# Decoder layer on one core: a weight block meets 520 tokens in matmuls of 402, 354, 284, 284 and 236 columns instead of six of 260

## What is computed

```python
xn = _rmsnorm(x, n_mix_pre)
q, fp, iv, og, lx, ly, ga, gb = jnp.split(xn @ w_in, idx, axis=-1)
f = lbh + (1.0 - lbh) * jax.nn.sigmoid(fp)
o, S_new = _hgrn2(silu(q), 1.0 - f, iv, jnp.log(f), S0, chunk)
o = o * lax.rsqrt(jnp.mean(o * o, axis=-1, keepdims=True) + EPS) * hg_onorm * silu(og)
out_a = o @ w_pa
xc, cbuf_new = _causal_conv(lx, cbuf, conv_w, conv_b)
h, h_last = _rglru(xc, xb @ wa + ba, xb @ wx + bx, log_lambda, h0, fresh)
out_b = (jax.nn.gelu(ly) * h) @ w_pb
merged = sigmoid(ga) * out_a + sigmoid(gb) * out_b
x = x + _rmsnorm(merged @ w_o, n_mix_post)
gate, up = jnp.split(_rmsnorm(x, n_ffn_pre) @ w_fi, 2, axis=-1)
x = x + _rmsnorm((silu(gate) * up) @ w_fo, n_ffn_post)
```

## Time and profile before

| | us |
|---|---|
| median of 3 runs | 1100.99 (1100.98 to 1101.19) |
| span of the profiled execution, first to last instruction | 1098.3 |
| TensorE busy, share | 1055.9, 96% |
| its weight loads | 1034.8, 94% |
| VectorE | 573.2, 52% |
| ScalarE | 434.1, 40% |

### The profile page before, as it was taken

One profiled execution on the slowest core, in us unless ns is written; L12 is line 12 of the kernel. 1 busy time (PEld: TensorE's weight loads), 2 busy tenths in 40 slices (PEclk: granted clock), 3 DMA queues, 4 the chain that ended last, 5 costly groups with the idle time before them and its releaser, 6 DMA issues.

```text
span 1098.3 us, 21670 instructions
## 1 busy us (share of the span) xinstructions
PE 1055.9 (96%) x8542; PEld 1034.8 (94%) x8542; DVE 573.2 (52%) x1028; ACT 434.1 (40%) x588; POOL 2.9 (0%) x9
## 2 busy tenths in 40 slices
PE   4899999999999999999999999699999999999997
PEld 3799999999999899999999999699999999999997
DVE  2666566657656788833333333855554554422223
ACT  5434335433442888822222233652323232322222
POOL 0000000000000000000000000000000000000000
PEclk9999999999999899999999999899999999999999
DMA  5533223222332233232333244033233323233321
GB/s 155 162 90 99 79 76 98 86 76 76 94 108 60 81 93 86 78 95 81 91 95 95 88 130 135 20 97 95 80 92 95 95 82 90 67 92 94 94 76 78
DMA packets 182881, 100.36 MB, mean 91 GB/s; under 512 B 3709, under 2 KB 181378, under 8 KB 182594
## 3 DMA queue, kind: packets, MB, share of 16 engines
q1 hardware_dynamic: 164898, 90.87, 27.8%
q10 hardware_dynamic: 17792, 8.91, 2.7%
q0 software_dynamic: 160, 0.15, 0.0%
HBM read 90.79 MB, written 9.13 MB: 91 GB/s over the span
## 4 chain that ended last, share of the span: by engine, by line
PE 90%; DVE 3%; ACT 2%; issue 1%; SPq 1%; DMA 1%; DVEq 0%; ACTq 0%
PE proj L1223 78%; PE pr L1322 5%; PE pi L1371 1%; DMA raw<-in_w_in 1%; PE pr L1376 1%; PE pi L1353 1%; PE pr L1345 1%; PE pi L1414 1%; PE pr L1414 1%; PE pi L1359 0%; ACT wh L358 0%; SPq L266 0%; DVE tmp L1122 0%; DVE acts L1110 0%; DVE raw L1202 0%
## 5 line engine op out<-in xcount | busy, mean ns | idle before, releaser
L1223 PE MATMUL proj<-acts,wh 128*128 128x260 f32 x4928 | 810.7, 287 | 15.5 <-DVE acts L1110 9.2
L1223 PEld LDWEIGHTS proj<-acts,wh 128*128 128x128 f32 x4928 | 679.9, 190 | 23.7 <-DVE acts L1110 10.8
L1223 PE MATMUL proj<-acts,wl 128*128 128x260 f32 x2464 | 498.5, 284 | 0.0
L1223 PEld LDWEIGHTS proj<-acts,wl 128*128 128x128 f32 x2464 | 381.9, 190 | 0.0
L720 DVE TENSOR_TENSOR wl<-raw,wh 128x1024 fp32r<-128x1024 f32 (+2 forms) x164 | 190.8, 1163 | 278.7 <-ACT wh L358 278.6
L358 ACT ACTIVATE wh<-raw 128x1024 fp32r<-128x1024 f32 (+2 forms) x164 | 165.6, 1010 | 358.9 <-PE proj L1223 350.5
L1322 PE MATMUL pr<-tmp 128*128 128x64 f32 (+1 forms) x512 | 66.4, 272 | 3.2 <-DVE tmp L947 3.2
L1322 PEld LDWEIGHTS pr<-tmp 128*128 128x128 f32 x512 | 62.9, 192 | 4.0 <-DVE tmp L947 3.4
L805 DVE TENSOR_TENSOR tmp<-tmp 128x256 f32<-128x256 f32 x56 | 23.6, 422 | 25.5 <-PE pr L1322 25.4
L676 ACT ACTIVATE acts<-tmp 128x520 f32 (+1 forms) x21 | 13.4, 639 | 42.4 <-DVE tmp L1170 42.4
L673 ACT ACTIVATE tmp<-tmp 128x520 f32<-128x520 f32 x21 | 13.5, 641 | 40.0 <-DVE tmp L1161 40.0
(11 more groups left out here) (239 smaller groups left out, 721.0 us busy)
## 6 DMA issues: line engine op xcount, KB each, us to landing
raw<-in_w_in SPq DMA_DIRECT2D x64, 512.0 KB, 4.0
raw<-in_w_ffn_in SPq DMA_DIRECT2D x44, 512.0 KB, 3.8
raw<-in_w_ffn_out SPq DMA_DIRECT2D x16, 384.0 KB, 3.1
raw<-in_w_ffn_out SPq DMA_DIRECT2D x16, 320.0 KB, 2.9
tmp<-in_state_hgrn ACTq DMA_DIRECT2D x8, 512.0 KB, 4.1
out<-tmp ACTq DMA_DIRECT2D x8, 512.0 KB, 3.2
raw<-in_w_branch_a SPq DMA_DIRECT2D x8, 512.0 KB, 3.6
raw<-in_w_branch_b SPq DMA_DIRECT2D x8, 512.0 KB, 3.5
```

The lines of the kernel that those rows point to most:

```text
L1223: o = mm(pp[par][:, hf, 0:TH], w, x[:, hf * TH:(hf + 1) * TH], start=start and n == 0, stop=stop and n == 2)
```

## The change

It cuts the 520 tokens at MA = 284 into an early part and a late part of MB = 236, twice MS = 118. A tile of activations with its low parts is now one row of 1040 columns: low parts of tokens 284 to 401 (118), the high parts (520), low parts of tokens 402 to 519 (118), low parts of tokens 0 to 283 (284). A matmul of 402 columns takes the first low piece with the early high parts, one of 354 the late high parts with the second low piece, one of 284 the early low parts; then the low weights meet the high parts in 284 and 236 columns. The results of the 236 late low columns land beside the others, in **side columns** of the bank pair (all four banks are one tensor now). They are added later: ScalarE's `keep_side` copies them to SBUF, VectorE's `gather` adds them to the late columns and says `summed`; all readers wait for that in place of `unit_done`.

A unit now does its eight k-tiles with the high weights first (waiting for `hi_ready` alone), then waits for `lo_ready` and does the eight with the low weights. A new word, `high_done`, falls between. ScalarE's prep waits for `high_done` and `lo_ready` of two units before, in place of `unit_done`; VectorE's prep waits for `unit_done` of two units before as well. The small matmuls stand at the same four points in the time of a unit. Low parts of activations are made by two VectorE instructions (284 and 2 x 118 columns) instead of one of 520. In the recurrent stage and the output projection ScalarE's prep is moved ahead of the reader of the unit. The masks are cast in one instruction of 576 columns, and broadcast where they are used.

```diff
+MA = 284
+MB = T - MA
+MS = MB // 2
+SW = MS + T
...
-        masks = sb("masks", [P, TP + (NLEV - 1) * TP // 2], U8)
+        masks = sb("masks", [P, MW], U8)
+        side = sb("side", [P, 2, MB])
...
                 if not isinstance(u, int) or u >= 2:
-                    eng.wait_ge(E("unit_done"), u - 1)
+                    eng.wait_ge(E("high_done"), u - 1)
+                    eng.wait_ge(E("lo_ready"), u - 1)
                 act(wh[:, s % 2, 0:nk], raw[:, s, 0:nk], AF.Copy).then_inc(E("hi_ready"), 1)
+            def keep_side(u, par, n=None):
+                n = u if n is None else n
+                eng.wait_ge(E("unit_done"), u + 1)
+                if not isinstance(n, int) or n >= 2:
+                    eng.wait_ge(E("summed"), n - 1)
+                act(side_copy(par), proj_side(par), AF.Copy).then_inc(E("side_kept"), 1)
...
+                    prep(u0 + 2 * bb + 1, 2 * bb + 1)
+                    keep_side(u0 + 2 * bb - 1, 1)
                     squares_of_ly(n - 1)
-                    prep(u0 + 2 * bb + 1, 2 * bb + 1)
                     gelu_tanh(n - 1)
                     branch_high(n - 2)
                     gates(n - 1)
                     prep(u0 + 2 * bb + 2, (2 * bb + 2) % 4)
+                    keep_side(u0 + 2 * bb, 0)
                     pre_conv(n, u0 + 2 * bb)
...
                 eng.wait_ge(E("hi_ready"), u + 1)
+                if not isinstance(u, int) or u >= 2:
+                    eng.wait_ge(E("unit_done"), u - 1)
                 tt(wl[:, s % 2, 0:nk], raw[:, s, 0:nk], wh[:, s % 2, 0:nk].bitcast(F32), SUB).then_inc(E("lo_ready"), 1)
+            def gather(u, par, n=None):
+                eng.wait_ge(E("side_kept"), (u if n is None else n) + 1)
+                eng.wait_ge(E("unit_done"), u + 1)
+                tt(proj_late(par), proj_late(par), side_copy(par), ADD).then_inc(E("summed"), 1)
+            def low_parts(reg, j, x):
+                h = hi_of(reg, j).bitcast(F32)
+                tt(lo_early(reg, j), x[:, 0:MA], h[:, 0:MA], SUB)
+                return tt(lo_late(reg, j), late(x), late(h), SUB)
...
-            for i in range(NLEV):
...
-                cp(mask(i).rearrange("p (c n) -> p c n", c=NCH), src).then_inc(E("m_made"), 1)
+            cp(masks[:], raw[:, 3].rearrange("p k n -> p (k n)")[:, 0:MW]).then_inc(E("m_made"), 1)
...
-            def ktile(s, par, reg, k, start, stop, koff=0):
...
+            def high_weights(s, par, reg, k, start, koff=0):
+                w = wh[:, s % 2, k, :]
+                columns(par, w, reg, koff + k, 0, MS + MA, -MA - MS, start, False)
+                columns(par, w, reg, koff + k, MS + MA, MB + MS, 0, start, False)
+                return columns(par, w, reg, koff + k, SW + MS, MA, -MA, False, False)
+            def low_weights(s, par, reg, k, stop, koff=0):
+                w = wl[:, s % 2, k, :]
+                columns(par, w, reg, koff + k, MS, MA, -MA, False, stop)
+                return columns(par, w, reg, koff + k, MS + MA, MB, 0, False, stop)
...
-                eng.wait_ge(E("lo_ready"), u + 1)
+                eng.wait_ge(E("hi_ready"), u + 1)
...
                 for k in range(nk):
                     if ready:
                         ready(k)
-                    o = ktile(s, par, reg, k, first and k == 0, last and k == nk - 1, koff)
+                    o = high_weights(s, par, reg, k, first and k == 0, koff)
+                    if k == nk - 1:
+                        o.then_inc(E("high_done"), 1)
+                    if k in (2, 5):
+                        for f in fill.get(k // 3, ()):
+                            f()
+                eng.wait_ge(E("lo_ready"), u + 1)
+                for k in range(nk):
+                    o = low_weights(s, par, reg, k, last and k == nk - 1, koff)
                     if k == nk - 1:
                         o.then_inc(E("unit_done"), 1)
```

More of the change, by code:

```diff
@@ L565, in _ @@
             first_tap(0)
+            prep(u0 + 3, 3)
             eng.wait_ge(E("p_os"), NH)
+            keep_side(u0 + 1, 1)
             squares_of_ly(0)
-            prep(u0 + 3, 3)
             squares(h)
@@ L573, in _ @@
             out_high(h)
+            prep(u0 + 4, 0)
+            keep_side(u0 + 2, 0)
             pre_conv(1, u0 + 2)
-            prep(u0 + 4, 0)
             gates(0)
@@ L593, in _ @@
                 ch.end(Q_LRU - 1)
+            prep(4 * G_MIX + 1, 1)
+            keep_side(4 * G_MIX - 1, 1)
             squares_of_ly(NH - 1)
-            prep(4 * G_MIX + 1, 1)
             gelu_tanh(NH - 1)
@@ L655, in _ @@
             prep(4 * G_FFI + 2, 2)
+            keep_side(4 * G_FFI, 0)
+            keep_side(4 * G_FFI + 1, 1)
             inverse_rms(1, 0)
@@ L670, in ffi @@
                     prep(u0 + 2 * jj + 2, (2 * jj + 2) % 4)
+                    keep_side(u0 + 2 * jj, 0)
                     eng.wait_ge(E("d_slr"), j)
@@ L913, in hg_steps @@
                 if prev:
+                    gather(4 * h - 1, 1)
                     prep(4 * h + 1, 1)
@@ L920, in hg_steps @@
                     level(h - 1, 7)
+                gather(4 * h, 0)
                 prep(4 * h + 2, 2)
@@ L928, in hg_steps @@
                     chunk_states(h - 1)
+                gather(4 * h + 1, 1)
                 prep(4 * h + 3, 3)
@@ L1018, in _ @@
             h, u0 = NH - 1, 4 * G_LRU
+            gather(u0 - 1, 1)
             prep(u0 + 1, 1)
@@ L1024, in _ @@
                 level(h, i)
+            gather(u0, 0)
             prep(u0 + 2, 2)
@@ L1029, in _ @@
             conv(0)
+            gather(u0 + 1, 1)
             prep(u0 + 3, 3)
@@ L1036, in _ @@
             head_low(h)
+            gather(u0 + 2, 0)
             prep(u0 + 4, 0)
@@ L1045, in _ @@
                     n = i * 2 + bb
+                    gather(u0 + 2 * bb - 1, 1)
                     gelu_inner(n - 1)
@@ L1051, in _ @@
                     gated(n - 1)
+                    gather(u0 + 2 * bb, 0)
                     prep(u0 + 2 * bb + 2, (2 * bb + 2) % 4)
@@ L1054, in _ @@
                 ch.end(Q_LRU - 1)
+            gather(4 * G_MIX - 1, 1)
             gelu_inner(NH - 1)
@@ L1060, in _ @@
             gated(NH - 1)
+            gather(4 * G_MIX, 0)
             prep(4 * G_MIX + 2, 2)
@@ L1101, in _ @@
                 for s in range(4):
+                    gather(4 * (G_OUT + i) + s, s % 2)
                     add_square(4 * i + s, s % 2, 2, 4 * i + s)
@@ L1215, in _, with columns @@
             mm = eng.matmul
-            def ktile(s, par, reg, k, start, stop, koff=0):
-                xh, xl = acts[:, reg[0] + koff + k], acts[:, reg[1] + koff + k]
-                a, b = wh[:, s % 2, k, :], wl[:, s % 2, k, :]
-                for n, (w, x) in enumerate(((a, xh), (a, xl), (b, xh))):
-                    for hf in range(2):
-                        o = mm(pp[par][:, hf, 0:TH], w, x[:, hf * TH:(hf + 1) * TH],
-                               start=start and n == 0, stop=stop and n == 2)
-                return o
+            def columns(par, w, reg, k, at, n, to, first, last):
+                mid = par * 1024 + 512 + to
+                return mm(pj[:, mid:mid + n], w, tile_cols(reg, k, at, n), start=first, stop=last)
+            def high_weights(s, par, reg, k, start, koff=0):
[7 more added lines that the diff above has]
+                return columns(par, w, reg, koff + k, MS + MA, MB, 0, False, stop)
             def unit(u, s, reg, fill=None, koff=0, nk=KT, par=None, free=None, first=True, last=True, ready=None):
                 par = s % 2 if par is None else par
-                eng.wait_ge(E("lo_ready"), u + 1)
+                fill = fill or {}
+                eng.wait_ge(E("hi_ready"), u + 1)
                 if free is not None:
```

189 lines of the change are left out of this document (117 added, 72 removed).

## The result

The changed kernel takes **1126.49 us** (1124.10 to 1127.54, 4 runs) against 1100.99 before; the ratio is 1.0231 (1.0219 to 1.0243). It is slower, as forecast, but by 25.5 us and not by 7.4, and outside the range given. The other three executions showed a mean granted clock of 0.989 to 0.991, this one 0.992, and took 1.5 to 3.4 us longer.

A forecast was written before the change was run, and what follows sets the result against it. TensorE's matmul stream, busy 96% of the span, was taken as the bound. Matmul savings of -6.5 us and costs elsewhere summed to +7.4 us on the median 1100.99, forecasting 1108.4 us, range 1071 to 1117.

The forecast's parts named there:

- Matmuls, -6.5 forecast: TensorE's stream: one matmul fewer per k-tile at equal columns saves 5.9 ns in 1104 k-tiles, -6.5 us.
- 8.2 ns a matmul: TensorE's pace: of 120.0 ns at 260 columns, 0.43 ns goes with each column and 8.2 ns with the matmul itself.
- rival B: TensorE's pace: the extra time goes with the columns, nothing gained, +13.9 us, 1114.9; chance 0.16.
- Rival A: TensorE's pace: a minimum per weight-load and matmul pair, hidden by wide matmuls, makes the kernel faster, 1074.7 us; chance 0.27.
- Recurrent stage, +8.0: Recurrent cycles: added passes make VectorE the bound, cycle 14.43 us against 13.28, +1.15 in each of 7, +8.0 us.
- Rival C: Recurrent cycle: waits overlap VectorE's work, so the stage costs nothing and keeps 0.8 us of gain, 1099.6; chance 0.12.
- Heads, +2.4: First stage, fourth level of eight heads: gather ahead of the split delays the score, 0.3 us each, +2.4 (0 to 4).
- Output projection +1.9: Output projection's first unit: TensorE waits for tile 7's low part, delayed by keep, gather and split, +1.9 us (0.8 to 2.5).
- mixer's start +1.3: Channel mixer's start: keeps, gathers and split low parts delay the copy that frees a bank, +1.3 us (0.5 to 2).
- Beginning -0.5: Kernel's beginning: eight mask casts of 1.76 us become one of about 0.45, one keep and gather come, -0.5 us.
- end +0.8: Kernel's end: keep and gather stand before the squares that the last sum waits for, +0.8 us.
- Cover: Mixer's steady units, mix and output projection: passes cost 0 because engines have time to spare; without it 0.8 us a unit.

The follow-up runs named there:

- experiment 1: Kernel before, matmuls of the later stages given other widths, a ladder from 128 to 512 columns; 112 ns at 128, 232 at 512, no total time given.
- experiment 6: Changed kernel with both side passes kept, but gather adds the side buffer to itself and readers wait only for the unit's end; 1111.53 us, ratio 1.0105.
- Experiment 8: Changed kernel with two orders altered: keep ahead of ScalarE's weight copy in the recurrent loop, first gather behind the heads' fourth level; 1125.91 us, ratio 1.0237.
- experiment 3: Kernel before with only the new unit order, all high weights first, then all low weights, six matmuls of 260 columns; 1100.20 us, ratio 0.9996.
- experiment 9: Kernel before with only the compact masks, one cast of 576 columns, broadcast when used; 1097.97 us, ratio 0.9971.

## Why the prediction was wrong

The sign and the largest mechanism were right: in the recurrent stage VectorE's queue became the bound, with TensorE idle before the odd unit and released by gelu. The size was not. Between the profiles 16.1 us are missing from the forecast's +7.4: 10.4 of them in the pace of the matmuls, 3.9 in the heads, 2.8 in the recurrent stage, 0.9 at the end, less 0.3 in the output projection and the mixer's start and 1.6 at the beginning. Step by step, against the table of stretches:

- **Matmuls, -6.5 forecast.** Measured +4: units 96 to 132, 288 k-tiles, take 208.56 us against 207.60, 3.3 ns more each, 4.1 us over all 1232. This is the step that failed most: "8.2 ns a matmul", of which the gain was to come. The forecast took the price per column, 0.43, from two durations behind a stall, rounded to 0.01 us; the ladder has 0.446, and what is left for a matmul shrinks from 8.2 to 4 ns, of which the floor takes back 3. The rival B, "with the columns", with 3 + 0.45 a column, was right, on the ground of the fp32 rows that had been set aside as another kind of operand. It had 720 for the changed k-tile; the 4 ns above that are seen beside unequal neighbours; experiment 1 shows those on the 284 behind a 236 apart from the changed kernel, and not those on the 354. Rival A, a minimum per pair that wide matmuls hide, is refuted: 402 columns take 183 and not 170.5. There is a minimum, but at 112.
- **Recurrent stage, +8.0.** Measured +11.35. Its terms: VectorE's work per cycle 12.98 forecast, 14.98 - 2.02 = 12.96 measured; waits 1.45 forecast, 2.02 measured in the longer cycle and 1.87 in the shorter. What was missing is the gather's wait for the keep, 0.29 or 0.14, since ScalarE's weight copy is put ahead of the keep, and 0.23 on the tap, where a small copy and two hand-overs stand between gather and tap. Outside the cycles the forecast had nothing. By TensorE's start times the pairs of units from 36 to 47 are 11.3 longer, units 48 to 51 1.7 and units 32 and 33 0.5, and units 34 and 35 are 2.2 shorter, by the wait and the clock told above. Rival C, that the waits would overlap, is refuted for the change as it is, and experiment 6 shows what it would need: that no reader waits for the gather.
- **Heads, +2.4.** Measured +6.90 in six heads, 1.15 each, 0.1 of it pace. The stall at level four was foreseen, with 0.3; the gap between starts is 0.35 longer than usual, and the forecast's bound was 4 for all eight heads. The second one, at the head's first score, was overlooked: the forecast looked at VectorE's slack and not at ScalarE's, whose sigmoid in front of a table load now waits for the gather. Experiment 8 shows that the stall at the levels is VectorE's load and not the gather's place, as far as two places show it.
- **Output projection +1.9, mixer's start +1.3.** Measured together +3.32, of which 0.4 is pace. That this is near the forecast is luck, since the parts are not. Tile 7 has its stall, 1.46 us and not 1.9, and 0.61 of it is there without side passes. The wait for the copy that frees a bank grew by 0.44 and not by 1.3. The sum behind the output projection waits 2.31 and not 1.43, which was not in the list, but the next wait is 0.73 shorter. The stalls before the mixer's tiles grew from 0.48 to 0.60; they are 0.60 without side passes too, and 0.48 in experiment 3, so the split low parts or the new cut make them and not the passes. The granted clock of the mixer's first two units (713.66 to 725.24, before 694.38 to 705.24) was lower as well: 0.80 against 0.86 in the mean.
- **Beginning -0.5, end +0.8.** The last sum waits 1.60 where it waited 0.76, the 0.8 forecast; the stretch is +1.80, of which 0.97 is there without side passes and was not taken apart. The beginning is -2.06; the chain of waits (after)

```profile
37.44 0.38 DVE masks L850
...
39.23 10.95 DMA raw<-in_w_in
```

has the cast at 37.44, and 1.38 us of the gain is the shorter cast, as with the masks alone (experiment 9). The rest is not seen in every kernel with these masks (91.15 and 92.34 in the table).
- **Cover.** In the mix and in the mixer the passes cost nothing, as forecast: the changed kernel and the one without side passes take the same 322.14 us there.

The terms as they came, with pace at 3.9 taken out of each stretch, are 10.8 recurrent, 6.3 heads, 2.9 output projection and mixer's start, 1.7 end, -2.1 beginning: the 23.5 us between the profiles. The range ended at 1117 because only the pace was taken at its worst in it. Even the forecast's own upper bounds, added up with no gain in pace (9.5 + 4 + 2.5 + 2 + 0.8 - 0.5 = 18.3), end at 1119.3: the pace was worse than its worst case, which had the k-tile unchanged, and so were the recurrent stage and the heads.

What stays open: why a column costs 0.446 ns at the full clock and not 0.417, where at half clock nothing is added; about 0.7 us of the gain at the beginning; and when the granted clock falls. No run here set the clock apart, and the shares put down to it rest on one profile of each kernel.

## To carry to other kernels

Before merging matmuls, measure the interval against the width: here it is 4 ns + 0.446 N above a floor of 112, so one matmul fewer at equal columns is worth 4 ns, and a cut that puts a matmul under the floor gives it back. A pass put between a unit and its readers costs its length, two hand-overs and whatever its own queue is doing at that moment. It was free here in the mix and the mixer, where the reader has a unit's time to spare; the stages with 0.1 to 0.5 us of slack paid, in each head and cycle, and in the cycles they paid for the waiting and not for the work. List all readers on both engines with the stage's slack, and keep such a pass out of the stages that are tight. Compare the granted clock of the same unit in both kernels before a difference is put down to an instruction.

## What the hardware showed unexpectedly

The matmul's interval is nearly a straight line from 260 to 512 columns, 120 to 232 ns, with a flat floor of 112 from 128 to 240. The floor is not of a single matmul but of a run: behind a 402 the 118 is over in 58 ns, and the next 402 takes 242.

TensorE's clock did not follow the length of a single wait. In the kernel before it fell to 0.50 at 356.1 behind a wait of 0.84 us and sixteen matmuls of one column; in the kernel without side passes waits of 2.07 us (until 371.71) and 1.92 us (until 378.57) left it at 1.00. That was no single case: the mean granted clock was 0.992 to 0.994 in all ten executions of that kernel, and 0.988 to 0.992 in those of the kernel before.
